# Sums of squares by high and low parts, gate functions in mid-pass, embedding operands in other buffers, and another order at the end of the mixers

## What is computed

```python
h = rms_norm(x, mix_norm_g)
dq, dk, dv, bq, bk, bv, z = split(h @ w_in)          # heads of 64, diff and dilated
dq, dk = rms_norm(dq), rms_norm(dk)                  # over the 64 of each head
a = diff_attention(dq, dk, dv, lam, slopes)          # softmax 0 - lam * softmax 1
a = rms_norm(a, diff_sub_norm_g) * (1 - lam_init)
bq, bk = rms_norm(bq), rms_norm(bk)
b = dilated_attention(bq, bk, bv, slopes)
y = concat(a, b) * silu(z)                           # the gates
x = x + y @ w_out
gate = sigmoid(rms_norm(x, ple_norm_g) @ w_ple_gate)
x = x + gate * (p @ w_ple_proj)                      # the embedding
```

## Time and profile before

| what | value |
|---|---|
| median of 3 runs | 2913.04 us (2912.51 to 2915.86) |
| the profiled execution's own time | 2912.82 us |
| its span | 2911.0 us |
| mean granted TensorE clock | 0.980 |
| TensorE busy | 2761.9 us, 95% |
| VectorE, ScalarE, GpSimd busy | 1708.0, 1045.7, 935.9 us |
| mixers, opening to last product | about 1890 to 2720 us |
| diff passes | 100 us each, dilated ones 85 us |

### The profile page before, as it was taken

One profiled execution on the slowest core, in us unless ns is written; L12 is line 12 of the kernel. 1 busy time (PEld: TensorE's weight loads), 2 busy tenths in 40 slices (PEclk: granted clock), 3 DMA queues, 4 the chain that ended last, 5 costly groups with the idle time before them and its releaser, 6 DMA issues. The chain is left out here.

```text
span 2911.0 us, 39453 instructions
## 1 busy us (share of the span) xinstructions
PE 2761.9 (95%) x15534; PEld 2115.5 (73%) x15534; DVE 1708.0 (59%) x2674; ACT 1045.7 (36%) x1735; POOL 935.9 (32%) x549
## 2 busy tenths in 40 slices
PE   6999999999999899999999999979999999998899
PEld 5879797977777677777766887755666666665677
DVE  5787878786022344444454115666776667775586
ACT  4342524343010233333333002346666644344232
POOL 1233323332664122211212334542122234341465
PEclk8999999999999899999999999989999999999999
DMA  4131413244432111111113225421110111103544
GB/s 166 60 84 66 94 66 83 71 80 155 165 118 91 37 52 52 50 47 48 34 44 135 82 80 183 137 86 36 40 43 27 43 43 44 43 30 113 173 150 112
DMA packets 113751, 237.32 MB, mean 82 GB/s; under 512 B 9120, under 2 KB 52896, under 8 KB 113568
## 3 DMA queue, kind: packets, MB, share of 16 engines
q1 hardware_dynamic: 63312, 172.93, 17.9%
q10 hardware_dynamic: 50256, 61.87, 7.3%
HBM read 190.66 MB, written 44.11 MB: 81 GB/s over the span
## 5 line engine op out<-in xcount | busy, mean ns | idle before, releaser
L79 PE MATMUL psum<-u_h,w_hi 128*128 128x512 f32 (+2 forms) x2624 | 1012.7, 386 | 25.0 <-PEq L46 7.3
L80 PE MATMUL psum<-u_h,w_hi 128*128 128x512 f32 (+2 forms) x2624 | 968.4, 369 | 0.0
L81 PE MATMUL psum<-u_h,w_lo 128*128 128x512 f32 (+2 forms) x2624 | 966.3, 368 | 0.0
L135 POOL TENSOR_SCALAR w_hi<-w_raw 128x1024 fp32r<-128x1024 f32 x212 | 241.6, 1140 | 1468.6 <-ACTq L1324 519.1
L79 PEld LDWEIGHTS psum<-u_h,w_hi 128*128 128x128 f32 x2624 | 497.8, 190 | 156.1 <-issue 69.3
L137 POOL TENSOR_TENSOR w_lo<-w_raw,w_hi 128x1024 fp32r<-128x1024 f32 x212 | 546.1, 2576 | 17.7
L81 PEld LDWEIGHTS psum<-u_h,w_lo 128*128 128x128 f32 x2624 | 497.8, 190 | 71.8
L80 PEld LDWEIGHTS psum<-u_h,w_hi 128*128 128x128 f32 x2624 | 498.5, 190 | 69.3 <-issue 9.0
L2545 ACT ACTIVATE a_exp<-a_exp 128x1024 f32<-128x1024 f32 x96 | 101.6, 1058 | 161.9 <-DVE a_exp L2708 88.3
L1349 ACT ACTIVATE f_exp<-psum 128x1024 f32<-128x1024 f32 (+4 forms) x112 | 82.2, 734 | 192.9 <-PE psum L1207 94.0
L1445 DVE CUSTOM_DVE_ANT_0 f_junk<-psum,f_decay,f_max 128x512 f32<-128x512 f32 (+2 forms) x96 | 60.3, 666 | 134.4 <-PE psum L1230 121.1
(11 more groups left out here) (433 smaller groups left out, 4419.3 us busy)
## 6 DMA issues: line engine op xcount, KB each, us to landing
w_raw<-in_w_all SPq DMA_DIRECT2D x212, 512.0 KB, 3.5
sums_rows<-s_acs ACTq DMA_DIRECT2D x32, 512.0 KB, 8.8
f_decay<-s_nc SPq DMA_DIRECT2D x16, 520.0 KB, 5.4
s_y<-conv_out ACTq DMA_DIRECT2D x16, 512.0 KB, 2.9
yo_raw<-s_y ACTq DMA_DIRECT2D x8, 1024.0 KB, 10.3
a_strips<-in_strips SPq DMA_DIRECT2D x8, 960.0 KB, 5.4
x_tok<-in_x SPq DMA_DIRECT2D x8, 512.0 KB, 8.2
s_xT<-xT SPq DMA_DIRECT2D x8, 512.0 KB, 6.0
```

The source lines that it names most:

```text
L79: nc.tensor.matmul(out, w_hi[:, k], a_hi, start=(k == 0 and first), stop=False)
L80: nc.tensor.matmul(out, w_hi[:, k], a_lo, start=False, stop=False)
L81: return nc.tensor.matmul(out, w_lo[:, k], a_hi, start=False, stop=(k == kk - 1 and final))
L135: self.nc.gpsimd.tensor_scalar(self.hi[:, r], self.raw[:, r], 1.0, 1.0, ALU.mult, ALU.mult).then_inc(self.hi_done, 1)
```

## The change

1. S for q = 0 to 4 (`halved`): ScalarE writes the rounded squares to `tok[:, 0]` instead of `sq`; GpSimd squares `un` in fp32 into `sq` and subtracts the rounded squares into `tok[:, 1]` (`squares_low`); TensorE adds two fp32r products with `exact`, a rounded copy of `K.pairs`, instead of one fp32 product. These S are late items: after the scores and two projection steps, and on ScalarE after `exps`. S for q = 5 to 7 stays.
2. `gates(p)` runs in pass p, unit 10 (diff) or 7 (dilated), instead of at the end of the pass before.
3. The embedding's weights go to `un` and `sq` instead of `junk` and `un`, and are loaded as soon as the last rows are split; p's last chunk goes to the second strips' free end, and p's loads wait less. Strips of dilated passes load 1536 of 1920 columns. On ScalarE `high_p` and `take_ple` come ahead of `exps`.
4. The last 16 steps run as tile 0 steps 0 to 6, tile 1 steps 0 to 3, tile 0 step 7, tile 1 steps 4 to 7.

```diff
+    halved = lambda q: q <= DIFF
-    is_late = lambda p, x, it: it[0] == "E" and x == 6 or it[0] in ("D", "P", "EB", "EP") or it[0] == "T" and (p < 0 or x == 13)
+    is_late = lambda p, x, it: it[0] == "S" and halved(it[1]) or it[0] == "E" and x == 6 or it[0] in ("D", "P", "EB", "EP") or it[0] == "T" and (p < 0 or x == 13)
...
-        pws = [junk, un[:, :, :].rearrange("p h c -> p (h c)")]
+        pws = [t[:, :, :].rearrange("p h c -> p (h c)") for t in (un, sq)]
-        p_in = lambda c: p_chunks[:, c] if c < CH - 1 else sq[:, 0, 0:2 * P]
+        p_in = lambda c: p_chunks[:, c] if c < CH - 1 else strips[:, 1, 1536:1536 + 2 * P]
...
-                sp.dma_start(strips[:, q % 2], K.d["strips"][q]).then_inc(strip_in[q % 2], 16)
+                n = SPAN if diff(q) else 1536
+                sp.dma_start(strips[:, q % 2, 0:n], K.d["strips"][q][:, 0:n]).then_inc(strip_in[q % 2], 16)
...
                 if p == LAST:
-                    sp.wait_ge(gfull, 8 * PASSES)
-                    sp.wait_ge(add_ok, base(LAST))
-                    sp.wait_ge(sfree, number[("EP", LAST, 0)] + 1)
                     sp.wait_ge(lo_ok, 4 * PASSES)
-                    tokens = K.d["p"][0, 0].rearrange("(c p) n -> p c n", p=P)
-                    sp.dma_start(p_chunks, tokens[:, 0:CH - 1]).then_inc(p_got, 16)
-                    sp.dma_start(p_in(CH - 1), tokens[:, CH - 1]).then_inc(p_got, 16)
                     for i in range(2):
                         src = K.d["w_ple"][4 * i:4 * i + 4].rearrange("f p k -> p f k")
                         sp.dma_start(pws[i].rearrange("p (f k) -> p f k", f=4), src).then_inc(w_got, 16)
+                    tokens = K.d["p"][0, 0].rearrange("(c p) n -> p c n", p=P)
+                    sp.dma_start(p_in(CH - 1), tokens[:, CH - 1]).then_inc(p_got, 16)
+                    sp.wait_ge(add_ok, base(LAST))
+                    sp.dma_start(p_chunks, tokens[:, 0:CH - 1]).then_inc(p_got, 16)
...
+            def squares_low(q, g):
+
+                c = number_of(q, g)
+                pool.wait_ge(sq_ok, c + 1)
+                pool.wait_ge(gfree, 8 * q + place(q, g) + 1)
+                nc.gpsimd.tensor_tensor(sq[:, c % 2], un[:, c % 2], un[:, c % 2], ALU.mult).then_inc(low_ok, 1)
+                pool.wait_ge(low_ok, 2 * c + 1)
+                nc.gpsimd.tensor_tensor(tok[:, 1, 512 * (c % 2):512 * (c % 2) + 512], sq[:, c % 2],
+                                        tok[:, 0, 512 * (c % 2):512 * (c % 2) + 512].bitcast(F32), ALU.subtract).then_inc(low_ok, 1)
...
                     if q < PASSES and x in normed_at(q):
                         split_rows(q, normed_at(q)[x])
+                    for g, k in share(q, x) if q < PASSES and halved(q) else []:
+                        if k == KT - 1 and g <= GQ1 and (q, g) != (0, GK1):
+                            squares_low(q, g)
+                    if (q, x) == (0, 5):
+                        squares_low(0, GK1)
...
             pool.wait_ge(w_got, 32)
+            pool.wait_ge(gfull, 8 * PASSES)
...
-                    pe.wait_ge(sq_ok, number_of(q, g) + 1)
-                    last = nc.tensor.matmul(bank, K.pairs[:, :], sq[:, number_of(q, g) % 2], start=True, stop=True)
+                    c = number_of(q, g)
+                    if halved(q):
+                        pe.wait_ge(const_ok, 1)
+                        pe.wait_ge(low_ok, 2 * c + 2)
+                        for i in range(2):
+                            last = nc.tensor.matmul(bank, exact, tok[:, i, 512 * (c % 2):512 * (c % 2) + 512], start=(i == 0), stop=(i == 1))
...
-            for ks in (range(LAST), [LAST]):
-                for u in range(2):
-                    W.wait(pe, 0, 0, 36 + u)
...
+            for u, ks in ((0, range(LAST)), (1, range(4)), (0, [LAST]), (1, range(4, KT))):
+                W.wait(pe, 0, 0, 36 + u)
...
-                    nc.scalar.activation(sq[:, c % 2], gbank(n), ACT.Square).then_inc(sq_ok, 1)
+                    squares = tok[:, 0, 512 * (c % 2):512 * (c % 2) + 512] if halved(q) else sq[:, c % 2]
+                    nc.scalar.activation(squares, gbank(n), ACT.Square).then_inc(sq_ok, 1)
...
-                    if X is not None:
-                        exps(X)
-                    if p == LAST and x in MIX_AT:
-                        high_mix(MIX_AT[x])
                     if p == LAST and x - 1 in TURN_AT:
                         high_p(TURN_AT[x - 1])
                     if p == LAST and x - 1 in PLE_AT:
                         for n in PLE_AT[x - 1]:
                             take_ple(n)
+                    if X is not None:
+                        exps(X)
+                    if p == LAST and x in MIX_AT:
+                        high_mix(MIX_AT[x])
...
-                    if x == 15 and q < PASSES:
-                        gates(q)
+                    if p >= 0 and x == (10 if diff(p) else 7):
+                        gates(p)
...
+            nc.vector.tensor_copy(exact, K.pairs[:, :])
```

More of the change, by code:

```diff
@@ L1901, in _, with mixers_phase @@
             split(KT - 1)
-def mixers_phase(nc, K, u_hi, u_lo, strips, pt, S, V_p, acc0, o1, x1, row_of):
+def mixers_phase(nc, K, u_hi, u_lo, exact, strips, pt, S, V_p, acc0, o1, x1, row_of):
     PASSES, DIFF, U, SPAN = 8, 4, 16, 2 * T - P
@@ L2026, in mixers_phase @@
         stored = [s(f"stored{i}") for i in range(4)]
-        tok_ok = s("tokens")
+        tok_ok, low_ok = s("tokens"), s("squares_low")
         rootx, invx, scalex, addx_ok, sqx_ok, sumx = (s(n) for n in ["rootx", "invx", "scalex", "addx", "sqx", "sumx"])
@@ L2260, in extra @@
                 if kind == "S":
-                    pe.wait_ge(sq_ok, number_of(q, g) + 1)
-                    last = nc.tensor.matmul(bank, K.pairs[:, :], sq[:, number_of(q, g) % 2], start=True, stop=True)
+                    c = number_of(q, g)
[4 more added lines that the diff above has]
+                            last = nc.tensor.matmul(bank, exact, tok[:, i, 512 * (c % 2):512 * (c % 2) + 512], start=(i == 0), stop=(i == 1))
+                    else:
+                        pe.wait_ge(sq_ok, c + 1)
+                        last = nc.tensor.matmul(bank, K.pairs[:, :], sq[:, c % 2], start=True, stop=True)
                 if kind == "N":
@@ L2450, in _ @@
             pe.wait_ge(add_ok, UNITS)
-            for ks in (range(LAST), [LAST]):
-                for u in range(2):
-                    W.wait(pe, 0, 0, 36 + u)
[L2454 to L2459, removed]
+            for u, ks in ((0, range(LAST)), (1, range(4)), (0, [LAST]), (1, range(4, KT))):
+                W.wait(pe, 0, 0, 36 + u)
+                for k in ks:
+                    if u == 0:
+                        pe.wait_ge(mix_lo, k + 1)
+                    last = gemm_k(nc, ps[:, 512 * u:512 * u + 512], W.hi[:, u], W.lo[:, u], u_hi[:, k, 0:512], u_lo[:, k, 0:512], k)
+                if u == 0 and LAST in ks:
+                    last.then_inc(gfull, 1)
         @block.scalar
@@ L3204, in program @@
                 W.base = W.base + 2 * KT
-                mixers_phase(nc, K, h_hi, h_lo, strips, pt, S, V_p, acc0, o1, x1, mix_row)
+                mixers_phase(nc, K, h_hi, h_lo, uh[:, 2 * KT * T:2 * KT * T + P], strips, pt, S, V_p, acc0, o1, x1, mix_row)
                 clear_semaphores(nc)
```

## The result

The changed kernel is slower: 2948.72 us, median of 4 runs (2946.68 to 2949.93), against 2912.78 (2912.19 to 2915.86) before; ratio 1.0121, 95% interval 1.0105 to 1.0137, or +35.9 us. The forecast was 2933 in a range to 2945: the direction was right, the time 3.7 us outside the range.

A forecast was written before the change was run, and what follows sets the result against it. The prediction took TensorE's instruction order inside a pass as the bound. Its terms, 30.1 - 6.9 + 2.1 + 0.5 - 3.1 - 2.1 = +20.6 us on a median of 2913.04, gave about 2933 us, range 2910 to 2945.

The forecast's parts named there:

- What bounds: Inside a mixer pass TensorE's instruction order sets the time, busy 99.04 of 100.00 us; any wait is paid in full.
- GpSimd's queue in the passes: Halves made by GpSimd come late for TensorE: +17.1 us over passes q = 1 to 3, +8 in q = 4.
- Both stalls: In a halved pass TensorE waits for GpSimd's halves: some 2 us at GQ0, 4 to 5 us at GQ1.
- My clock term: Low granted clock after the stall before GQ1 costs TensorE 1.0 us in each pass.
- The port: Two-input VectorE operations stand still until GpSimd's ends, so a pass costs 4.7 us; without that, 2.8.
- Rival 2: No port effect: the moved weight split doesn't hold VectorE's scaling; passes cost 1.6 to 2.8 us, about 2914; chance 0.18.
- rival 3: GpSimd's halves cost half and arrive before TensorE, so squares are hidden: about 2894 us; chance 0.10 with milder mixtures.
- Rival 4: Both stalls of each halved pass bring low clock in full: 8 us more, about 2941; chance 0.10.
- The opening: At q = 0 GpSimd's halves delay the row for the first key tile, partly fitting idle time: +5 us, ends 2 and 8.
- Part 2: Gates moved mid-pass: -6.9 us of waits at dilated boundaries, +2.1 in diff passes at unit 10, +0.5 in dilated unit 7.
- Parts 3 and 4: Embedding's buffers and ScalarE's order in the last pass: -3.1 us; last steps reordered, freeing GpSimd's final split sooner: -2.1 us.
- case 1: GpSimd's queue and port delay GQ1's halves in every halved pass: about 2933 us, span 2920 to 2941; chance 0.62.

The follow-up runs named there:

- e7: Changed kernel with the weight split of unit 4 put behind GQ1's squares (unit 6) in the halved passes; 2957.76 us, ratio to before 1.0158.
- e4: Changed kernel with the opening's first weight split ahead of GQ0's squares in GpSimd's queue instead of behind; 2940.49 us, ratio to before 1.0096.
- e13: Changed kernel, but in the opening (q = 0) both products read the rounded squares and GpSimd does nothing for them; 2932.50 us, ratio to before 1.0073.
- e9: Version of e1 with the gates back at each pass's end; 2907.00 us, ratio to before 0.9979.
- e1: Changed kernel without halves: all sums of squares as one fp32 product at the old place, other parts kept; 2902.54 us, ratio to before 0.9965.
- e12: Version of e1 with gates mid-pass in dilated passes only, at the pass's end in diff passes; 2901.82 us, ratio to before 0.9962.
- e2: Changed kernel with gates, ScalarE's order in the last pass and last steps put back; halves, new buffers and loads stay; 2957.72 us, ratio 1.0152.
- e5: Changed kernel without GpSimd's two operations per sum: both products read the rounded squares, low parts left out; 2896.85 us, ratio to before 0.9947.
- e15: Changed kernel with fp32 squares in the opening and GQ1's squares ahead of GQ0's rows in unit 6; 2911.18 us, ratio to before 0.9999.

## Why the prediction was off

- **What bounds: right.** A wait within a diff pass is paid in full: 1.66 + 1.12 + 3.28 us of waits, 1.5 of low clock and 0.7 for the gates, less 2.0 gained by the products, are 6.3 of the 6.8 us by which a pass is longer than the 99.8 of before. The open 0.5 I can't place.
- **GpSimd's queue in the passes: right, forecast 17.1 and 8, measured 18.9 and 8.1.** Both stalls are where they were put, 1.66 (said "some 2") and 3.28 (said 4 to 5). My clock term, 1.0, was 1.5; the wait for query rows, 1.12, I had not seen. So the sum came this close partly by luck, since these errors offset the shorter stall. GpSimd's multiply took 1.04 us, nearer my 1.3 than the 0.61.
- **The port: right.** e7 and the two L2813 rows show 2.7 us. Rival 2, 2914, falls by them; rival 3 falls by the waits. Rival 4's low clock comes after the stall at GQ1; the 2 us after GQ0's stall stayed at 1.00, so it isn't "both stalls".
- **The opening: the failed step.** "I take +5, ends 2 and 8" measured 18 to 19. It looked at the first key tile alone, and let GpSimd's new work "fit into its idle time". But GpSimd's idle time there is a wait at the head of its queue: `squares_low(0, GQ0)` in unit 1 holds the opening's first weight split until ScalarE has copied GQ0, and TensorE needs those weights sooner (e4: 7.0 us by trace, 8.2 by median, with the clock). I had named what is queued behind the halves for unit 4 and unit 6, not for units 0 and 1. A second piece, that S(GQ1) falls behind the first key tile and its scaling ahead of the second maxima, I had seen; my term had 3.8 us for the halves ahead of the rows and so 1.2 for this. Measured are some 6 to 8 and 2 to 5 (e13), so both were short, and the queue had nothing.
- **Part 2: right.** Forecast 6.9 - 2.6 = 4.3; e9 less e1 is 4.5 by median and 3.9 by trace up to the next phase. The waits of 1.5 and 3.0 went. Up to the last pass it was worth more, 6.4, and there 2.5 of it were lost again to later waits, which the forecast didn't count. Gates at unit 10 cost 0.7 a pass, as forecast (e12). A stretch of low clock behind the second 1.5 us wait (granted 0.53 from 2556.5 to 2560.0 us before) is not the gates' doing: in e9 and e2, with the gates back, the same waits of 1.46 and 0.69 us stand there and the clock behind them is 1.00 (2559.5 to 2563.0 and 2599.8 to 2603.3 us).
- **Parts 3 and 4.** 3.1 forecast, 1.9 to 2.4 by trace: more of it fell into the last waits for denominators, L2275 up to 3.4 us from 3.0. 2.1 forecast, 3.4 by trace: 2.0 at the border, the rest the clock, 0.66 over the next phase's first 5 us against 0.50.
- Parts 2 to 4 together: forecast -9.5, e1 -9 to -10 by median and ratio, but -14.3 by its trace from the mixers' start. Some 5 of these aren't owed to the gates, ScalarE's order or the last steps, since e2, without them, has the same 1.5 and 3.4 us by a higher clock at equal waits. So that the last line of the table meets its forecast (-8.0 for -8.2) is partly luck. Whether the new buffers and loads, which e2 keeps, raise the clock there, or chance does, wasn't tested.
- The range: the lower ends of case 1's terms, 3 x 1.6 + 3.5 + 2 - 9.5 = 0.8, give 2914 and not 2920. The upper end held 8 us for the opening, and that is the end that broke. Of the 15.7 us missed, 13 to 14 are the opening's.

## What to carry to other kernels

An engine's idle time is free for new work only if nothing stands behind the instruction that it idles at. For each new instruction that waits, name the next one in that queue and who needs it, in the prologue too, where operands come in another order and a stage is longer. And a cheaper product on the bounding engine (9.8 us here) wasn't worth two operations on an engine that feeds it: rounded squares alone, at no cost to GpSimd (e5, sums not exact), gained 6 us of 2903; halves made by GpSimd lost 46, and with the queue mended in two places (e15) still some 9.

## What the hardware showed that was not expected

That VectorE stands still beside GpSimd was in the prediction, but not for an instruction so small: a VectorE subtraction of 128x8 elements took 2.235 us instead of 0.167 beside GpSimd's 2.4 us subtraction, so the loss is set here by GpSimd's instruction and not by VectorE's own size. GpSimd's product of a tile with itself took 1.04 us where its subtraction of two tiles of the same 128x512 took 1.26 to 1.30; the outputs' types differ as well (fp32 and fp32r), so the reason stays open. After waits of the same length, 1.46 and 0.69 us, the granted clock was 0.53 in one profiled execution and 1.00 in two others. And code that no edit touched, all ahead of the mixers, ended up to 5 us apart from one profiled execution to another, which is as much as parts 3 and 4 are worth; shifts between two fixed places of a trace were needed to size them.
